# Rotary tables copied per block into DRAM, and a longer hold on addresses that stores read, in a decoder layer on eight cores

## The chip, the cores and the metric

The kernel runs on one Trainium2 chip, on 8 cores. Each core computes one sequence of the batch of eight; no core speaks to another. A core has five engines with a queue of instructions each: TensorE (PE, matrix products), VectorE (DVE), ScalarE (ACT), GpSimd (POOL) and SyncE (SP, which only issues transfers here), and 16 DMA engines that carry the transfers. Engines meet by semaphores. The metric is the device time in microseconds of the slowest core.

## The reference

One decoder layer for x of 4096 x 1024 per sequence, with a condition c that gives shifts, scales and gates (adaLN). A combined input projection feeds latent attention (8 heads, 96 = 64 plain + 32 rotary dimensions) and retention (4 heads), an output projection follows, then a SwiGLU feed-forward of width 2816.

```python
mod = (jax.nn.silu(c) @ w_ada[l] + b_ada[l])[:, None, :]
sh1, sc1, g1, sh2, sc2, g2 = jnp.split(mod, 6, axis=-1)
h = rmsnorm(x, pre_norm_mix[l]) * (1.0 + sc1) + sh1
z = h @ w_in[l]
cq, ckv, kpe, rq, rk, rv, rg = jnp.split(z, offsets, axis=-1)
y_mla = rmsnorm(mla_group(cq, ckv, kpe, positions, ...), mla_out_norm[l])
y_ret = retention_group(rq, rk, rv, rg, positions, ret_gn_gain[l])
mix = jnp.concatenate([y_mla, y_ret], axis=-1) @ w_out[l]
x = x + g1 * rmsnorm(mix, post_norm_mix[l])
h = rmsnorm(x, pre_norm_ffn[l]) * (1.0 + sc2) + sh2
f = (jax.nn.silu(h @ w_gate[l]) * (h @ w_up[l])) @ w_down[l]
x = x + g2 * rmsnorm(f, post_norm_ffn[l])
```

The part that the change touches is the rotary embedding of the queries. With cos and sin of position times frequency it is

```python
x1, x2 = jnp.split(x, 2, axis=-1)
jnp.concatenate([x1 * cos - x2 * sin, x1 * sin + x2 * cos], axis=-1)
```

## The kernel before

The sequence is cut into 8 blocks of 512 rows, and a block into 4 tiles of 128 rows. The program has three stages.

Projections: for `sb` from 0 to 7, `prep` loads and normalises four tiles of x (`xt`, `xn`) and turns them (`hT`), `z_part` multiplies them by the input weights `W1` (in the trace W and w) and forms per tile `cqn`, `ckn`, `kpn`, the rotated retention inputs (`r1`, `r2` in VectorE, both `r` in the trace, summed to `rqk`), `rv` and the gate (`th`, then `sg`). `latents` turns them and stores `cqT`, `ckT` and `kpT` to scratch in DRAM. `retention` of the block before runs between the tiles and stores `yn` to `yg_scr`, 128x512 f32, 256 KB a tile. `ada_chunk` computes one piece of the adaLN vectors per block from a 1 MB load `wadab`.

Attention: blocks in the order 6, 7, 5, 4, 3, 2, 1, 0. Keys are made from `ckTb` (loaded from `ck_scr`, a ring of 3) by `kgen`; queries of the next block by `qgen`, one of the fill steps between the score products. ScalarE takes the exponentials `PT`. Output projections of the block before fill the rest.

Feed-forward: blocks in the same order, products of `h2T` with `Wg`, `Wu`, and of `h1T` with `Wd`.

The rotary table of the queries: `angles` makes for all 4096 positions three tiles of 128x512 f32 (256 KB each), `fC` (cosine), `fS` (sine), `fN` (minus sine). Partition 16b + i holds frequency i for the 512 positions of block b. Each is stored whole to `tab_scr`. For a block, `load` in `qgen` fills `Cq` and `Sq`, 128x512 each: partition 32h + 16k + i is head h of four, half k, frequency i. For `Cq` both halves are the cosine, for `Sq` minus sine and sine. The table in DRAM has the 16 rows of a block once, so each of the two tiles is filled by 8 transfers of 16x512 (32 KB). `pe_part` multiplies two products by the two tables (`qt`, on VectorE), adds them (`qp`, on GpSimd), and four transfers carry the heads into `Q`.

Order and addresses: `record` writes the program down as a list of operations with the tiles that each reads and writes. From a first recording each tile has a life, from the first to the last operation that names it (`_touch`), and `_place` gives it an address in 212,800 bytes per partition: pinned and fixed tiles first, then by class (`cls`) and size. Small short-lived tiles are put where the addresses have been free for `GAPCAP` = 40 operations, if there is such a place. It tries seeds with random jitter until ten plans fit; each is recorded and ordered once, and the plan whose ordering the scheduler's cost table makes shortest is taken. `_list_schedule` orders each engine's queue with the same cost table: of the operations that are ready, the one recorded first. When a tile begins its life, its first writer waits for every operation that read or wrote a tile which had the same address (`b.alias`); for a tile that a transfer stores to DRAM that is the landing of the store. SyncE has 32 semaphores; its transfer number n (from 0) uses semaphore `ds_sp` n mod 32.

Of the kernel before, what the change touches and what calls it, by code (L numbers as in the profile page):

```python
# [9 lines left out]
F32 = mybir.dt.float32  # L10
# [10 lines left out]
NSB = 8  # L21
# [127 lines left out]
class Buf:  # L149
    def __init__(self, name, size, kind):  # L150
        self.name = name
        self.size = size
        self.kind = kind
        self.addr = 0
        self.first = None
        self.last = None
        self.whole = [None, []]
        self.subs = {}
        self.seen = False
        self.pin = False  # L160
        self.alias = None


class Sched:
# [61 lines left out]
    def op(self, eng, emit, r=(), w=(), dma=False):  # L226
        op = Op()
        op.eng = eng
        op.emit = _freeze(emit)
        op.is_dma = dma  # L230
        op.marked = False
        op.count = 0
        op.seq = len(self.order)
        d = set()
        rl = [k if isinstance(k, tuple) else (k, None) for k in r]
        wl = [k if isinstance(k, tuple) else (k, None) for k in w]
        for b, _ in rl + wl:
            self._touch(b, op.seq)

        def need(st, write, psum):  # L240
            if st[0] is not None:
                d.add(st[0])
            if write:
                d.update(st[1])
            elif psum:
                d.update(x for x in st[1] if x.eng != eng)

        for lst, write in ((rl, False), (wl, True)):
            for b, s in lst:
                ps = b.kind == "psum"  # L250
                need(b.whole, write, ps)
                if b.alias and b.whole[0] is None and (s is None or s not in b.subs or b.subs[s][0] is None):
                    d.update(b.alias)
                if s is None:
                    for st in b.subs.values():
                        need(st, write, ps)
                elif s in b.subs:
                    need(b.subs[s], write, ps)
        for b, s in rl:
            if s is None:  # L260
                b.whole[1].append(op)
            else:
                b.subs.setdefault(s, [None, []])[1].append(op)
        for b, s in wl:
            if s is None:
                b.whole = [op, []]
                b.subs = {}
            else:
                b.subs[s] = [op, []]
        d.discard(op)  # L270
        op.deps = d
        self.order.append(op)
        return op
# [8 lines left out]
    def _place(self, seed):  # L282
        rng = np.random.default_rng(seed)
        n = len(self.order)
        for b in self.bufs:
            if b.first is None:
                b.first = b.last = 0
            if b.pin:
                b.first, b.last = 0, n

        def cls(b):
            if b.pin or b.fix is not None:
                return -1 if b.fix is not None else 0
            if seed % 8 > 3 and b.last - b.first > 2000:
                return 0
            return 1 if b.last - b.first > (1000, 500, 1500, 250)[seed % 4] else 2

        jit = 1.0 + (0.5 * rng.random(len(self.bufs)) if seed else np.zeros(len(self.bufs)))
        order = sorted(self.bufs, key=lambda b: (cls(b), -b.size * (jit[b.no] if cls(b) == 1 else 1.0), b.first, b.no))
        m = len(order)  # L300
        A0, A1, L0, L1 = (np.zeros(m, np.int64) for _ in range(4))
        for i, b in enumerate(order):
            a0, a1, l0, l1 = A0[:i], A1[:i], L0[:i], L1[:i]
            live = (l0 <= b.last) & (l1 >= b.first)
            if b.fix is not None:
                b.addr = b.fix
                if (live & (a0 < b.addr + b.size) & (b.addr < a1)).any():
                    return f"{b.name} [{b.first},{b.last}] is not free at {b.addr}"
                A0[i], A1[i], L0[i], L1[i] = b.addr, b.addr + b.size, b.first, b.last
                continue  # L310
            cur, holes = 0, []
            for lo, hi in sorted(zip(a0[live].tolist(), a1[live].tolist())):
                if lo - cur >= b.size:
                    holes.append((cur, lo))
                cur = max(cur, hi)
            if ARENA - cur >= b.size:
                holes.append((cur, ARENA))
            if not holes:
                return f"no room for {b.name} {b.size} [{b.first},{b.last}]"
            near = (~live) & (l1 > b.first - GAPCAP) & (l0 < b.last + GAPCAP)  # L320
            na0, na1 = a0[near], a1[near]
            ngap = np.where(l1[near] < b.first, b.first - l1[near], l0[near] - b.last)
            edges = np.unique(np.concatenate([na1, na0 - b.size, a0[~live], a1[~live] - b.size]))
            best = None
            for lo, hi in holes:
                pts = np.unique(np.concatenate([[lo, hi - b.size], edges[(edges >= lo) & (edges <= hi - b.size)]]))
                if cls(b) == 2 and len(na0):
                    hit = (na0[None, :] < pts[:, None] + b.size) & (pts[:, None] < na1[None, :])
                    gap = np.minimum(np.where(hit, ngap[None, :], GAPCAP).min(axis=1), GAPCAP)
                else:  # L330
                    gap = np.full(len(pts), GAPCAP)
                edge = np.minimum(pts - lo, hi - b.size - pts)
                k = np.lexsort((pts, edge, -gap))[0]
                sc = (-int(gap[k]), int(edge[k]), int(pts[k]))
                if best is None or sc < best:
                    best = sc
            b.addr = best[2]
            A0[i], A1[i], L0[i], L1[i] = b.addr, b.addr + b.size, b.first, b.last
        plan = []
        for b in self.bufs:  # L340
            hit = (L1 < b.first) & (A0 < b.addr + b.size) & (b.addr < A1)
            over = sorted(order[k].no for k in np.nonzero(hit)[0])
            plan.append((b.addr, over))
        return plan
# [147 lines left out]


GAPCAP = 40


def bcast(v, dims):
# [6 lines left out]
def record(nc, S, dr, arena, psum):  # L504
# [249 lines left out]
    act(fS.v, fs_.v, AF.Sin, [fs_], [fS])  # L754
    act(fN.v, fs_.v, AF.Sin, [fs_], [fN], scale=-1.0)
    tabD = S.key("tabD")
    for i, t_ in enumerate((fC, fN, fS)):
        dma("sp", dr["tab"][i], t_.v, r=[t_], w=[(tabD, i)])

    Wvf = S.buf("Wvf", 2 * 512)  # L760
    dma("sp", Wvf.v.rearrange("p (c n) -> p c n", c=2), dr["wkv"][:, 512:1024].rearrange("(c p) n -> p c n", p=128), w=[Wvf])
# [263 lines left out]
    def qgen(s, engs=("dve", "dve")):  # L1025
# [11 lines left out]
        def load():  # L1037
            box["C"] = rg["Cq"]()
            box["S"] = rg["Sq"]()
            for k, o in (("C", [0, 0]), ("S", [1, 2])):  # L1040
                for hf in range(2):
                    for hd in range(4):
                        p0 = hd * 32 + hf * 16
                        dma("sp", box[k].v[p0:p0 + 16, :], dr["tab"][o[hf]][s * 16:(s + 1) * 16, :], r=[(tabD, o[hf])], w=[(box[k], p0)])

        def pe_part(q4):
            def a():
# [49 lines left out]
    for sb in range(NSB):  # L1097
        R = {}
        if sb > 0:
            ada_load(ada_list[sb])  # L1100
        if sb + 1 < NSB:
            hT2, xst, trs = prep(sb + 1, load_x(sb + 1))
        zset[0] = (2, 3, 4, 5, 6, 7) if sb == 0 else (2, 3, 4, 5, 6)
        zg = [z_part(sb, hT, R, j) for j in range(4)]
        for j in range(4):
            if j == 3 and sb + 1 < NSB:
                trs()
            for _ in range(4):
                for g_ in (zg if sb == 0 else zg[j:j + 1]):
                    next(g_, None)  # L1110
                if sb == 0:
                    break
            if prev:
                retention(*prev, j)
            if sb == NSB - 1:
                early_keys(j)
            if sb == 0 and j == 1:
                ada_load(ada_list[0])
            if j < 2 and sb + 1 < NSB:
                xst(2 * j)  # L1120
                xst(2 * j + 1)
        if sb == NSB - 2:
            first.extend(qgen(order[0], AD))
            first[1][0]()
        ada_chunk(ada_list[sb])
        if sb == 5:
            b_weights()
        res = []
        lat = latents(sb, R, res)
        if sb + 1 < NSB:  # L1130
            for _ in lat:
                pass
            prev = (sb, R) + tuple(res)
        hT = hT2
# [314 lines left out]
def build_nc():  # L1449
# [30 lines left out]
    dr["cqT"] = nc.dram_tensor("cq_scr", [NSB, 128, 3 * 512], BF16).ap()  # L1480
    dr["ckT"] = nc.dram_tensor("ck_scr", [NSB, 128, 2 * 512], BF16).ap()
    dr["kpT"] = nc.dram_tensor("kp_scr", [32, T], BF16).ap()
    dr["tab"] = nc.dram_tensor("tab_scr", [3, 128, 512], F32).ap()

    with contextlib.ExitStack() as ctx:
        arena = ctx.enter_context(nc.sbuf_tensor("arena", [128, ARENA // 4], F32))
# [113 lines left out]
```

How the kernel before makes its waits and increments, by code:

```python
    def then_inc(self, *a, **kw):  # L145
        return self
# [324 lines left out]
        def run(e, engobj):  # L471
            for op in self.ops[e]:
                for d in op.waits:
                    if d.is_dma:
                        n = NSEM[d.eng]
                        engobj.wait_ge(dsem[d.eng][d.dma_i % n], 16 * (d.dma_i // n + 1))
                    else:
                        engobj.wait_ge(esem[d.eng], d.count)
                ins = op.emit(engobj)
                if op.is_dma:
                    ins.then_inc(dsem[e][op.dma_i % NSEM[e]], 16)
                elif op.marked:
                    if ins is None:
                        ins = engobj.nop()
                    ins.then_inc(esem[e], 1)
```

## Time and profile before

| | us |
|---|---|
| median of 3 runs | 2051.67 |
| lowest, highest | 2024.93, 2135.98 |
| profiled execution | 2027.99 |
| its span (slowest core, core 2) | 2026.4 |
| spans of the eight cores | 2005.9 to 2026.4 |
| TensorE busy | 1854.3 (92%) |
| ScalarE busy | 965.1 (48%) |
| VectorE busy | 808.4 (40%) |
| GpSimd busy | 627.1 (31%) |
| moved by DMA | 189.71 MB, mean 94 GB/s |

The page divides the span into engine times, a chain of work that ended last, and groups of instructions. The chain lies 71% on TensorE, 9% on DMA, 8% on ScalarE and 3% on SyncE's queue; the store of `yn` to `yg_scr` alone has 3% of it. The mean granted clock of TensorE is 0.984 on the slowest core and 0.984 to 0.989 over the eight. Idle time is read as "idle before an instruction, and who released it"; a wait for several semaphores is put down to the one that came last.

### The profile page before, as it was taken

What the parts mean: (1) busy time and instruction counts of PE and PEld (TensorE: products, weight loads), DVE (VectorE), ACT (ScalarE), POOL (GpSimd) and SP (SyncE); (2) the same over time, 40 slices, a digit from 0 to 9 for tenths busy, and PEclk for the clock granted to TensorE, in tenths of its full rate; (3) what the DMA queues carried; (4) which work ended last, traced back from release to release, by engine and by line L of the source; (5) the groups of instructions that cost most, each with busy time, mean ns of one, the idle gap of its engine ahead of it and who ended that gap; (6) DMA issues with size and microseconds to landing.
All of it is one profiled execution on the core that took longest, in us unless ns stands there. A gap on an engine that the chain in (4) does not pass through costs nothing.

```text
span 2026.4 us, 38698 instructions; the slowest of 8 cores (2005.9 to 2026.4 us)
## 1 busy us (share of the span) xinstructions
PE 1854.3 (92%) x13325; PEld 973.1 (48%) x13536; DVE 808.4 (40%) x1733; ACT 965.1 (48%) x1449; POOL 627.1 (31%) x939
## 2 busy tenths in 40 slices
PE   1799988979989899999989999999999999999998
PEld 1355545535555555565544444444444444444443
DVE  4455655555444143545785423131221313122111
ACT  3566666539989999998741122121211212121111
POOL 3345546531523133435673330120302021020202
PEclk9999999989999999999989999999999999999999
DMA  9945445453323233254488621120202011120101
GB/s 251 170 97 127 124 119 139 85 117 90 94 79 105 40 100 88 82 121 129 121 196 180 161 97 44 52 73 22 104 11 83 32 57 68 42 84 22 53 22 63
DMA packets 91495, 189.71 MB, mean 94 GB/s; under 512 B 9640, under 2 KB 39976, under 8 KB 91304
## 3 DMA queue, kind: packets, MB, share of 16 engines
q1 hardware_dynamic: 62392, 157.02, 24.5%
q0 software_dynamic: 28912, 30.21, 9.9%
q8 instruction: 112, 1.84, 0.4%
q14 instruction: 79, 0.65, 0.1%
HBM read 167.34 MB, written 47.97 MB: 106 GB/s over the span
## 4 chain that ended last, share of the span: by engine, by line
PE 71%; DMA 9%; ACT 8%; issue 5%; SPq 3%; DVE 2%; POOL 1%; DVEq 0%; POOLq 0%; ACTq 0%
PE bank L541 69%; ACT PT L517 7%; DMA yg_scr<-yn 3%; SPq L514 3%; PE bank L548 2%; DMA W<-w 2%; DMA waf<-w_ada 1%; DMA yg<-yg_scr 1%; DMA xa<-x_scr 0%; ACT yn L517 0%; DMA ckTb<-ck_scr 0%; DMA cq_scr<-cqT 0%; POOL yn L520 0%; DVE mo L533 0%; DVE Q L533 0%
## 5 line engine op out<-in xcount | busy, mean ns | idle before, releaser
L517 ACT ACTIVATE PT<-bank 128x1024 bf16<-128x1024 f32 (+1 forms) x538 | 516.8, 1012 | 62.5 <-PE bank L541 51.1
L541 PE MATMUL bank<-Q,KT 96*128 96x512 bf16 (+3 forms) x1152 | 319.1, 364 | 27.0 <-ACT PT L517 13.2
L517 ACT ACTIVATE sgt<-bank 128x512 bf16<-128x512 f32 x176 | 104.8, 597 | 491.9 <-PE bank L541 445.7
L541 PE MATMUL bank<-h2T,Wg 128*128 128x512 bf16 x1396 | 332.7, 380 | 3.6 <-ACT sgt L517 2.5
L541 PE MATMUL bank<-h2T,Wu 128*128 128x512 bf16 x1357 | 326.8, 379 | 2.6
L541 PEld LDWEIGHTS bank<-V,PT 128*128 128x128 bf16 x4224 | 235.4, 97 | 173.5 <-issue 13.0
L541 PE MATMUL bank<-Wd,h1T 128*128 128x512 bf16 x1382 | 306.3, 379 | 1.7 <-DVE mo L533 0.4
L520 DVE TENSOR_TENSOR h1T<-bank,sgt 128x512 bf16<-128x512 f32 x176 | 121.3, 690 | 427.7 <-PE bank L541 396.4
L541 PE MATMUL bank<-W,hT 128*128 128x512 bf16 (+2 forms) x1252 | 257.5, 358 | 25.7 <-DVE r L520 8.8
L541 PE MATMUL bank<-V,PT 128*128 128x65 bf16 x4224 | 268.6, 193 | 6.3 <-POOL PT L520 2.9
L541 PEld LDWEIGHTS bank<-h2T,Wg 128*128 128x128 bf16 x1408 | 137.4, 98 | 168.6 <-issue 5.9
L541 PEld LDWEIGHTS bank<-Wd,h1T 128*128 128x128 bf16 x1408 | 137.6, 98 | 166.3 <-issue 0.9
L541 PEld LDWEIGHTS bank<-h2T,Wu 128*128 128x128 bf16 x1408 | 137.4, 98 | 164.2
L520 POOL TENSOR_TENSOR st<-st 128x1 f32<-128x1 f32 x32 | 6.2, 195 | 605.3 <-ACT t L517 605.3
L541 PEld LDWEIGHTS bank<-W,hT 128*128 128x128 bf16 x1280 | 123.5, 100 | 139.2 <-issue 40.1
L517 ACT ACTIVATE t<-bank 128x512 f32<-128x512 f32 x64 | 38.2, 597 | 276.7 <-PE bank L541 236.9
L520 POOL TENSOR_TENSOR PT<-PT,trib 128x256 bf16<-128x256 bf16 (+1 forms) x160 | 94.6, 595 | 236.1 <-ACT PT L517 232.0
L541 PE MATMUL bank<-Wo,yT 128*128 128x512 bf16 x461 | 141.2, 381 | 4.5 <-ACT PT L517 1.4
L528 DVE SCALAR_TENSOR_TENSOR t<-bank,st,G2b 128x512 f32<-128x512 f32 x64 | 45.1, 746 | 235.8 <-POOL st L520 235.8
L541 PEld LDWEIGHTS bank<-Q,KT 96*128 96x128 bf16 x1152 | 80.9, 97 | 62.1 <-issue 45.9
L520 POOL TENSOR_TENSOR xt<-xt,mo 128x512 f32<-128x512 f32 x64 | 88.2, 1394 | 25.1 <-DVE mo L528 24.3
L520 POOL TENSOR_TENSOR xb<-xb,t 128x512 f32<-128x512 f32 x64 | 80.6, 1281 | 28.2 <-DVE t L528 27.6
(160 smaller groups left out, 1847.0 us busy)
## 6 DMA issues: line engine op xcount, KB each, us to landing
xt<-x SPq DMA_DIRECT2D x64, 512.0 KB, 5.4
x_scr<-xt SPq DMA_DIRECT2D x32, 512.0 KB, 2.7
xa<-x_scr SPq DMA_DIRECT2D x32, 512.0 KB, 4.5
xb<-x_scr SPq DMA_DIRECT2D x32, 512.0 KB, 3.5
out<-xb SPq DMA_DIRECT2D x32, 512.0 KB, 2.6
waf<-w_ada SPq DMA_DIRECT2D x4, 2048.0 KB, 21.1
wadab<-w_ada POOLq DMA_DIRECT2D x8, 1024.0 KB, 14.2
yg_scr<-yn SPq DMA_DIRECT2D x32, 256.0 KB, 3.1
```

The source lines that it names most:

```text
L514: return OP(q, lambda g: g.dma_start(out=out, in_=in_), r, w, dma=True)
L517: return OP("act", lambda g: g.activation(out=out, in_=in_, func=func, **kw), r, w)
L520: return OP(eng, lambda g: g.tensor_tensor(out=out, in0=a, in1=b, op=op), r, w)
L528: return OP("dve", lambda g: g.scalar_tensor_tensor(out=out, in0=a, scalar=sc, in1=b, op0=op0, op1=op1), r, w)
L541: x = g.matmul(out, lhsT=l, rhs=rh, start=st, stop=sp, **kw)
L548: x = g.transpose(out=out, in_=i, identity=identb.v)
```

## The change

Three things change. The table in DRAM becomes two tables of 8 blocks x 128 rows x 512, in the layout of `Cq` and `Sq`; `store_tables` fills them by 16 stores of 8 x 16 x 512 (256 KB each), from the same three tiles, which are kept until then. It is recorded in block 2 and names a part of `V1` as read, so it can't run before that part of block 1 is written. `load` takes each table of a block with one transfer of 128x512. And a tile whose last use is a transfer that reads it keeps its address for `STORE` = 60 more operations of the list. The class by which large long-lived tiles are placed is also split in two by size for some seeds.

```diff
+        if dma:
+            for b, _ in rl:
+                b.stored = op.seq
...
             if b.pin:
                 b.first, b.last = 0, n
+            elif b.stored == b.last:
+                b.last = min(n, b.last + STORE)
+                b.stored = -1
...
             if seed % 8 > 3 and b.last - b.first > 2000:
-                return 0
+                return 0.25 if b.size >= 8192 else 0.5
...
+STORE = 60
...
-    for i, t_ in enumerate((fC, fN, fS)):
-        dma("sp", dr["tab"][i], t_.v, r=[t_], w=[(tabD, i)])
+    def store_tables():
+        for k, hf, t_ in ((0, 0, fC), (0, 1, fC), (1, 0, fN), (1, 1, fS)):
+            for hd in range(4):
+                dma("sp", bass.AP(dr["tab"].tensor, (k * NSB * 128 + hd * 32 + hf * 16) * 512, [[128 * 512, NSB], [512, 16], [1, 512]]), t_.v,
+                    r=[t_, (Vt[1], 3)], w=[(tabD, (k, hf, hd))])
...
-            for k, o in (("C", [0, 0]), ("S", [1, 2])):
-                for hf in range(2):
-                    for hd in range(4):
-                        p0 = hd * 32 + hf * 16
-                        dma("sp", box[k].v[p0:p0 + 16, :], dr["tab"][o[hf]][s * 16:(s + 1) * 16, :], r=[(tabD, o[hf])], w=[(box[k], p0)])
+            for i, k in enumerate("CS"):
+                dma("sp", box[k].v, dr["tab"][i, s], r=[tabD], w=[box[k]])
...
+        if sb == 2:
+            store_tables()
...
-    dr["tab"] = nc.dram_tensor("tab_scr", [3, 128, 512], F32).ap()
+    dr["tab"] = nc.dram_tensor("tab_scr", [2, NSB, 128, 512], F32).ap()
```

SyncE's queue at the end of block 1, before. The names are the stores of `latents` and `retention` and the loads of x:

```order
L514 DMA yg_scr<-yn 128x512
L514 DMA ck_scr<-ckT 128x1024
L514 DMA cq_scr<-cqT 128x1536
L514 DMA xt<-x 128x1024
L514 DMA kp_scr<-kpT 32x512
L514 DMA yg_scr<-yn 128x512 x3
```

and of the changed kernel at the same place:

```order
L522 DMA yg_scr<-yn 128x512
L522 DMA ck_scr<-ckT 128x1024
L522 DMA tab_scr<-fC 8x16x512
L522 DMA cq_scr<-cqT 128x1536
L522 DMA tab_scr<-fC 8x16x512
L522 DMA kp_scr<-kpT 32x512
L522 DMA tab_scr<-fC 8x16x512 x6
L522 DMA tab_scr<-fN 8x16x512
L522 DMA yg_scr<-yn 128x512
L522 DMA tab_scr<-fN 8x16x512 x3
L522 DMA tab_scr<-fS 8x16x512 x4
L522 DMA yg_scr<-yn 128x512 x2
```

The sixteen table stores stand in between, nine of them ahead of the first `yn` store of the next tiles. The three stores of before stood ahead of the x loads of block 1.

VectorE's queue in the first tile of block 2, before. `r1_291` and `r2_292` are the two rotary products; semaphore 9 of SyncE is there that of transfer 41, the store of `yn_270`:

```order
L520 TENSOR_TENSOR r1_291<-bank1,Ct_95 128x512 [waits es_pe]
L520 TENSOR_TENSOR rv_286<-bank1,wk_81 128x512 [waits es_pe,ds_sp18]
L524 TENSOR_SCALAR ckn_283<-bank3,lst_281 128x256 [waits es_pool]
L520 TENSOR_TENSOR scm_294<-bank2,Dm_80 128x512 [waits es_pe]
L528 SCALAR_TENSOR_TENSOR sg_287<-th_293,bank2 128x512 [waits es_act,ds_sp23]
L520 TENSOR_TENSOR r2_292<-bank1,St_96 128x512 [waits ds_sp9]
```

and of the changed kernel:

```order
L528 TENSOR_TENSOR r2_292<-bank1,St_96 128x512 [waits es_pe]
L528 TENSOR_TENSOR kp1_289<-bank3,Ct_95 128x32 [waits es_act]
L528 TENSOR_TENSOR kp2_290<-bank3,St_96 128x32
L528 TENSOR_TENSOR rv_286<-bank1,wk_81 128x512 [waits es_pe]
L532 TENSOR_SCALAR ckn_283<-bank3,lst_281 128x256 [waits es_pool]
L528 TENSOR_TENSOR r1_291<-bank1,Ct_95 128x512 [waits ds_sp2]
```

`r2_292` no longer waits for a transfer; `r1_291` now waits for one, number 34, the store of `yn_252`, one tile older. On ScalarE the next tile's `th_313` waited for TensorE alone and now also for transfer 47 (semaphore 15), the store of `yn_270`:

```order
L525 ACTIVATE xn_279,xst_320<-xt_278 128x1024 [waits ds_sp31]
L525 ACTIVATE yn_298<-bank3,gs_297 128x128 [waits es_dve]
L525 ACTIVATE yn_298<-bank3,gs_297 128x128 x3
L525 ACTIVATE th_313<-bank3 128x512 [waits es_pe,ds_sp15]
L525 ACTIVATE xn_279<-xt_277,xst_319 128x1024 [waits es_act,es_pool]
```

## Rows read from the trace of the kernel before

**Rows 1.** Part 1 of the page: busy us, share of the span, instructions, by engine.

```profile
PE 1854.3 (92%) x13325; PEld 973.1 (48%) x13536; DVE 808.4 (40%) x1733; ACT 965.1 (48%) x1449; POOL 627.1 (31%) x939
```

**Rows 2.** Core 2 by stage: length; PE, PEld, DVE, ACT, POOL busy; clock; DMA share; GB/s.

```profile
0.00:90.00 90.00, 32.30 (x286) 19.82 (x288) 42.63 (x72) 40.49 (x65) 32.87 (x50) 0.99 1.01 230
...
145.00:370.00 225.00, 201.71 (x1453) 115.51 (x1474) 129.04 (x402) 141.14 (x298) 124.57 (x208) 0.97 0.48 124
...
370.00:470.00 100.00, 78.94 (x513) 40.33 (x520) 57.50 (x151) 49.65 (x100) 38.92 (x55) 0.91 0.50 109
...
470.00:1060.00 590.00, 542.59 (x6144) 328.77 (x6223) 295.11 (x617) 519.28 (x560) 237.17 (x330) 0.98 0.39 104
...
1165.00:1990.00 825.00, 820.89 (x3912) 380.90 (x3989) 192.66 (x294) 159.24 (x322) 120.06 (x192) 1.00 0.16 54
```

**Rows 3.** Waits, 90 to 450 us: total us, times, longest.

```profile
DVE r L520 <- DMA yg_scr<-yn: 13.4, 4, 4.2
...
PE bank L541 <- DVE r L520: 8.8, 6, 2.6
...
ACT xn L517 <- DMA kp_scr<-kpT: 8.8, 2, 5.2
...
ACT xn L517 <- DMA cq_scr<-cqT: 7.2, 3, 3.1
...
ACT yn L517 <- DMA yg_scr<-yn: 6.5, 3, 4.8
...
POOL Wq L525 <- DMA yg_scr<-yn: 5.1, 1, 5.1
```

**Rows 4.** Timeline, VectorE and TensorE: start, us, instruction, [idle before <- releaser].

```profile
162.96 0.69 DVE L520 TENSOR_TENSOR r<-bank,St 128x512 f32<-128x512 f32 x1 [3.07 <-DMA yg_scr<-yn]
...
163.79 5.89 PE L541 MATMUL bank<-W,hT 128*128 128x384 bf16 x32 [1.81 <-DVE r L520]
```

**Rows 5.** The chain of work that ended last, 150 to 170 us: start, us, what.

```profile
156.68 6.18 DMA yg_scr<-yn
```

**Rows 6.** Timeline of SyncE's queue, 405 to 442 us.

```profile
420.16 5.26 SPq L514 DMA_DIRECT2D Cq<-tab_scr  x8
...
425.56 0.31 SPq L514 DMA_DIRECT2D Sq<-tab_scr  x1
...
428.53 2.85 SPq L514 DMA_DIRECT2D Sq<-tab_scr  x6
...
431.88 0.43 SPq L514 DMA_DIRECT2D Sq<-tab_scr  x1
...
441.65 0.35 SPq L514 DMA_DIRECT2D ckTb<-ck_scr  x1
```

**Rows 7.** Timeline of TensorE, 395 to 470 us.

```profile
441.65 1.87 PE L541 MATMUL bank<-ckTb,Wk 128*128 128x512 bf16 x4 [3.33 <-DMA ckTb<-ck_scr]
...
445.92 1.01 PE L541 MATMUL bank<-ckTb,Wk 128*128 128x512 bf16 x2 [2.41 <-DVE KT L533]
...
449.84 4.03 PE L541 MATMUL bank<-ckTb,Wk 128*128 128x512 bf16 x10 [2.91 <-DMA ckTb<-ck_scr]
```

**Rows 8.** Timeline of the head: SyncE's first table store, TensorE's last wait.

```profile
63.76 0.33 SPq L514 DMA_DIRECT2D tab_scr<-fS  x1
...
90.14 7.70 PE L541 MATMUL bank<-W,hT 128*128 128x512 bf16 x24 [6.03 <-DMA W<-w]
```

**Rows 9.** Busy time of the stage from 80 to 90 us, columns as in rows 2.

```profile
80.00:90.00 10.00, 4.06 (x19) 1.67 (x17) 2.07 (x3) 6.58 (x10) 4.32 (x10) 0.91 1.05 254
```

**Rows 10.** DMA issues, 90 to 450 us: count, KB each, median us to landing.

```profile
yg_scr<-yn SPq DMA_DIRECT2D x27, 256.0 KB, 4.4
```

**Rows 11.** The tile Sq: who waited for it (us, times).

```profile
  DVE qt L520: 5.8, 1
```

**Rows 12.** Timeline of SyncE's queue and ScalarE in the second block.

```profile
149.50 0.33 SPq L514 DMA_DIRECT2D ck_scr<-ckT  x1
...
171.98 0.61 ACT L517 ACTIVATE th<-bank 128x512 f32<-128x512 f32 x1
...
188.69 0.82 SPq L514 DMA_DIRECT2D xt<-x  x2
```

More of the change, by code:

```diff
@@ L161, in __init__ @@
         self.alias = None
+        self.stored = -1
 class Sched:
```

## The prediction

> **What bounds the kernel now.** I read the busy shares first, then the busy time by stage, then the waits and the timeline of the stages in which TensorE stands idle. TensorE is busy in 92% of the span [rows 1]. By stage [rows 2], it is busy 820.89 of the last 825 us, so nothing can pay there; before that its idle time is 57.7 us in the first 90 us (loads of weights), 225 - 201.71 = 23.3 us from 145 to 370 (the projections and the retention), 100 - 78.94 = 21.1 us from 370 to 470 (the last projection block and the start of attention), and 47.4 us in the 590 us of attention that follow, where ScalarE is itself busy 519.28 us of 590, so that a table load moved there can give little. The granted clock is 0.97 and 0.91 in the two stages that the change touches most.
>
> In the projection stage other engines wait for stores to land [rows 3]: VectorE's rotary products 13.4 us in four waits, ScalarE 8.8, 7.2 and 6.5 us, GpSimd 5.1 us, 41 us in all. They aren't data waits: the waiting instruction writes an address which a store still reads. TensorE in turn waits for VectorE's `r` 8.8 us in six waits. One of them in full [rows 4, 5]: the store of `yn` is issued at 156.68 and takes 6.18 us; the `r` product starts at 162.96 after 3.07 us of idleness, and TensorE at 163.79 after 1.81 us. So a 3 us wait on VectorE cost TensorE about 1.8.
>
> At the start of attention SyncE's queue is a chain of issues [rows 6]: from 420.16 on eight pieces of Cq (5.26 us), one of Sq (0.31), six more (2.85) and so on, with other issues between, until the key latent load goes out at 441.65. TensorE waits 3.33, 2.41 and 2.91 us there [rows 7], two of the three directly for such loads.
>
> **The change, part by part.** The sum is made against the profiled execution, 2028.0 us (span 2026.4), which lies 24 us under the median of the three runs (2051.67) and 3 us above the fastest (2024.93).
>
> *Three table stores leave the head.* They were 0.79 MB, issued from 63.76 on, in a stage in which the DMA engines are busy without a break until the last projection weight lands at 90.14 [rows 8]. At the 254 GB/s of the last ten microseconds [rows 9], 0.79 MB is 3.1 us. Against it, the x loads of the next blocks no longer stand behind ScalarE's sines and can start sooner; two more of them (1.0 MB) ahead of the weights would cost 4.1 us. Gain 2; bounds 3.1 gained and 1.0 lost.
>
> *Addresses are held for sixty more instructions.* The reuse that followed a store by some forty recorded instructions now follows it by at least a hundred, in a stage that records about sixty instructions per 128 rows and spends 225 us on some twenty such tiles, about 11 us each. A store lands in 4.4 us in the median there [rows 10], so the shortest reuses go from under to over its landing. Of the 41 us, nearly all should go; TensorE can regain what it waits for `r`, 8.8 us at most directly, and not all its 23.3 us of idleness, of which the rest ends on products, transposes and norms. By the ratio of [rows 4] I take 6 us. The clock at 0.97 over 225 us means some 13 us at the lower level (1.2 of 2.4 GHz), which cost half of that; fewer gaps may give back 2. Gain 8; bounds 0 and 23.3 + 6.7 = 30.
>
> *Two table loads instead of sixteen per block.* Bytes stay (2 x 256 KB). SyncE saves 14 issues a block. In the stage of [rows 6] sixteen pieces take 5.26 + 0.31 + 2.85 + 0.43 (the last piece) = 8.85 us of the queue, two whole loads 0.7, so what stands behind them can go 8 us sooner, and the stores of `yn` that SyncE and ScalarE wait for there fall out too. TensorE's three waits sum to 8.65 us; with part of it tied to the copies between, I take 5, and 2 for the clock (0.91 over 100 us is 18 us at the lower level, which cost 9). Gain 7; bounds 0 and 21.1 + 9 = 30. Later in attention the only wait for a table is VectorE's 5.8 us, once [rows 11], with none on TensorE behind it: gain 1, bounds 0 and 5.8. Where a whole load replaces the piece that an early product needed, nothing is lost, since the product reads all 128 partitions anyway.
>
> *Sixteen stores of 256 KB in the second block.* They write 4.19 MB in place of 0.79. In the new order the first ones stand right behind the ck store, which was issued at 149.50 [rows 12], the bulk behind the kp store, and nine of them ahead of the store of `yn_270`, whose address ScalarE's `th_313` now reuses. At 254 GB/s one takes 1.03 us. The seven behind the kp store, queued from about 153.3 on, end at 160.5, and with 4.4 us for its own way the `yn` store is down at 164.9. `th` of that tile ran at 171.98 [rows 12]. So it is covered by 7 us, and all sixteen are through by about 171, before the next x loads (188.69). SyncE's extra sixteen issues (5 us at 0.33 each) lie in a stretch where it waits for `yn`. I take a cost of 1; bounds 0 and, if every one took the 4.4 us of [rows 10] in turn, ten (with the `yn` store itself) x 4.4 = 44 us, landing at 193.5 and 22 late.
>
> *The address plan* is drawn anew and moves the order of single instructions on all engines. I see no row that prices this; it is worth nothing either way in the sum, and in the range up to the 9 us that all waits for `r` make.
>
> Sum: -2 - 8 - 7 - 1 + 1 = -17 us, 2028 - 17 = **2011 us**.
>
> **The rivals.**
>
> *A: the new stores run on half of the DMA engines* (0.17). Each goes out as 8 blocks x 16 rows on the DRAM side, where all the old ones had 128 rows outermost. At half rate one takes 2.06 us, seven end at 153.3 + 14.4 = 167.7, the `yn` store lands at 172.1, level with `th`'s old time and up to 8 us behind it where the tiles ahead have moved up. ScalarE's queue, with the norms and casts behind it, would stand for 0 to 8 us, and the `w_ada` load meanwhile shares the loaded engines. Cost 4 more: 2015 us. No row here shows a transfer of this shape with its landing. The Trainium skill, "DMA: Bandwidth & Descriptors", section on why a DMA increments its semaphore by 16, states that the slowest dimension of both sides sets how many engines take part, which here would be 8. By that rule the sum would be 2015, by the rate of the rows 2011; no run here has shown it yet.
>
> *B: the waits only change their name* (0.22). For it speaks that in 145 to 370 only 8.8 of 23.3 idle us are behind `r`, and that several store waits lie on ScalarE beside other waits. A freed engine then stops at the next product, and the key loads at the start of attention wait for their rings instead. Gain 2 of the head at most, 2026 us.
>
> *C: the gaps go as a whole* (0.15). The chain of waits passes through stores again and again in the first stages; if two thirds of 23.3 + 21.1 us vanish (-30) and half of the clock's 16 us comes back (-8), it is 1990 us.
>
> *D: slower* (0.08). The mechanism is the queue of sixteen stores alone: in turn at 4.4 us each, `th_313` stands 22 us, and x loads issued behind them come late into the same gap. 2011 - 1 + 22 = 2032, with a gain of only half elsewhere 2040. It decides from 18 us of lateness on, which is (171.98 + 18 - 149.5) / 10 = 4.0 us a store.
>
> **How the numbers follow.** Forecast 0.38, A 0.17, B 0.22, C 0.15, D 0.08. The likeliest is 2011, its own range 1998 to 2024. The range from 1988 to 2042 takes in A and B, most of C, and D up to near its upper end; it also holds executions a little above the profiled one, as one of the three runs was. Two per cent is about what a measurement of this kernel can tell from no change. Against the profiled time the line is 1987, below which only part of C lies; against the median it is 2011, and which of these the comparison comes near depends on its runs. I give 0.17 for faster, 0.04 for slower (D with a mean start), 0.79 between.
>
> **What would show it.** In the profile after: VectorE's and ScalarE's waits for yg, cq and kp stores between 90 and 450 us under 12 us in all (they were 41); TensorE's idleness from 145 to 370 about 16 us and the clock at 0.98 or more; W's last wait ended near 88 us; the key latent loads at the start of attention issued 6 to 8 us sooner by the same mark and TensorE's idleness in those 100 us near 15; a wait of ScalarE's `th` for the yn store near 165 us absent (present means A or D, and the landing of the table stores tells which). The forecast is wrong if idleness in these stages stays within 5 us of what it was, or if it falls but attention, with the redrawn plan, takes it back.

## The result, and the profile after

The changed kernel takes 2012.13 us in the median, against 2027.94 for the kernel before, measured beside it. The ratio is 0.9936, 95% interval 0.9918 to 0.9955: faster, by less than 2%. The forecast was 2011 us. The number was right, in part by luck: several of its terms were not, and another address plan of the same kernel comes out near 1995 us, as shown below.

| | before | after |
|---|---|---|
| median, us | 2027.94 | 2012.13 |
| profiled execution | 2027.99 | 2021.09 |
| spans of cores 0 to 3 | 2007.7 to 2026.4 | 1987.7 to 2003.0 |
| moved by DMA, MB | 189.71 | 193.10 |

In 8 of the 18 executions of after that the ratio counts, the profiled one among them (there on cores 4 to 7), some cores ran at a granted clock of 0.968 to 0.976 and took longer, so all rows of after are from cores 0 to 3, and the other ten executions have a median of 2006.6 us. The view by core has the span and clock:

```profile
core 2: 1988.1 us, clock 0.988
...
core 7: 2017.6 us, clock 0.973
```

Core 2 by stage, the same view as in [rows 2]. The columns are length; PE, PEld, DVE, ACT and POOL busy with instruction counts; clock; DMA share; GB/s:

```profile
0.00:90.00 90.00, 37.43 (x300) 21.56 (x301) 42.28 (x73) 41.83 (x67) 28.28 (x52) 0.97 1.01 233
145.00:370.00 225.00, 209.36 (x1553) 120.01 (x1551) 135.35 (x426) 148.00 (x314) 130.87 (x215) 0.98 0.51 142
370.00:470.00 100.00, 85.15 (x642) 44.09 (x641) 62.74 (x137) 60.63 (x101) 31.05 (x46) 0.93 0.45 113
470.00:1060.00 590.00, 556.62 (x6167) 331.61 (x6165) 302.74 (x637) 503.06 (x545) 248.07 (x344) 0.99 0.43 112
1135.00:1960.00 825.00, 825.00 (x3991) 380.81 (x3989) 192.48 (x294) 159.35 (x324) 118.42 (x197) 1.00 0.16 54
```

TensorE's idleness on this core went from 23.3 to 225 - 209.36 = 15.6 us in the projections, from 21.1 to 14.9 at the start of attention, and from 47.4 to 33.4 in attention. The last is the largest fall, in the stage to which the prediction gave 1 us.

The waits for stores from 90 to 450 us on core 2, the same view as in [rows 3] (total us, times, longest), are these two:

```profile
ACT xn L525 <- DMA ck_scr<-ckT: 4.5, 3, 2.1
...
ACT th L525 <- DMA yg_scr<-yn: 3.6, 1, 3.6
```

and one of VectorE's `r` of 0.8 us: 8.9 us, where there were 41. TensorE's 8.8 us of waits for `r` are gone.

**A ledger that doesn't depend on the clock time.** Fixed windows cut the two programs at different work. So I also read at what time TensorE starts its weight load number n. There are 13,536 of them on each core and in every kernel here. Number 500 lies in the second block, 3000 in the first attention block, 9000 near the end of attention; the end is the last weight load. Medians, us from one mark to the next, over the eight cores before and over cores 0 to 3 after:

| | 0 to 500 | 500 to 3000 | 3000 to 9000 | 9000 to end |
|---|---|---|---|---|
| before | 116.8 | 369.3 | 572.7 | 944.2 |
| after | 115.3 | 365.5 | 561.0 | 942.4 |
| difference | -1.5 | -3.8 | -11.7 | -1.8 |
| predicted | -2 | -14 | -1 | 0 |

Over cores 0 to 3 on both sides the differences are -1.6, -5.1, -12.6 and -2.0.

Cores of one execution do the same work, yet from 500 to 3000 they differ by 8 us before (368.2 to 376.0) and by 10 after (360.2 to 370.4). Core 2 went from 376.0 to 360.2, so it alone would suggest a gain of 16 us where the medians give 4.

### The profile page after: what moved, and what is told of

Same layout as the page of the kernel before. It is cut to its first block, busy times and chain, and to the rows that moved or that the text cites. A ratio compares the mean times of both kernels' runs of the same rounds, so it can differ in the third digit from the quotient of the medians.

```text
span 2019.5 us, 38646 instructions; the slowest of 8 cores (1987.7 to 2019.5 us)
## 1 busy us (share of the span) xinstructions
PE 1883.3 (93%) x13536; PEld 979.8 (49%) x13536; DVE 809.6 (40%) x1733; ACT 966.3 (48%) x1449; POOL 615.9 (30%) x939
## 2 busy tenths in 40 slices
DMA packets 91445, 193.10 MB, mean 96 GB/s; under 512 B 7928, under 2 KB 38264, under 8 KB 91256
## 4 chain that ended last, share of the span: by engine, by line
PE 77%; ACT 8%; DMA 7%; issue 3%; SPq 2%; DVE 1%; POOL 1%; POOLq 0%; ACTq 0%; DVEq 0%
PE bank L549 75%; ACT PT L525 7%; PE bank L556 2%; DMA W<-w 2%; SPq L522 2%; DMA yg_scr<-yn 1%; DMA waf<-w_ada 1%; DMA ckTb<-ck_scr 1%; DMA xt<-x 0%; DMA xa<-x_scr 0%; DMA ck_scr<-ckT 0%; DMA bb<-b_ada 0%; DMA wstage<-wq 0%; DVE Q L541 0%; DVE mo L541 0%
## 5 line engine op out<-in xcount | busy, mean ns | idle before, releaser
L549 PE MATMUL bank<-h2T,Wu 128*128 128x512 bf16 x1408 | 332.6, 379 | 0.0
L549 PE MATMUL bank<-W,hT 128*128 128x512 bf16 (+2 forms) x1280 | 277.6, 376 | 20.3 <-DMA W<-w 7.4
L549 PEld LDWEIGHTS bank<-W,hT 128*128 128x128 bf16 x1280 | 128.5, 103 | 144.3 <-issue 69.5
L549 PE MATMUL bank<-Wo,yT 128*128 128x512 bf16 x512 | 159.0, 385 | 2.4 <-DVE mo L541 1.2
L533 POOL TENSOR_SCALAR xst<-xst 128x1 f32<-128x1 f32 x64 | 12.5, 195 | 256.9 <-ACT xn L525 255.3
```

The lines of the kernel that those rows point to most:

```text
L533: return OP(eng, lambda g: g.tensor_scalar(out=out, in0=a, scalar1=s1, scalar2=s2, op0=op0, op1=op1), r, w)
L549: x = g.matmul(out, lhsT=l, rhs=rh, start=st, stop=sp, **kw)
```

## The experiments

Twelve kernels ran, each against the kernel before on the same chip. The marks are medians over eight cores, for the change and for "both" over cores 0 to 3. "Store waits" are the waits of all engines for the stores of `yn`, `cqT`, `ckT` and `kpT` from 90 to 450 us, lowest and highest of cores 0 to 3.

| kernel | ratio, interval | 500 to 3000 | 3000 to 9000 | store waits |
|---|---|---|---|---|
| before | 1 | 369.3 | 572.7 | 35 to 44 |
| before, other plan | 0.996 (0.9945, 0.9975) | 368.0 | 572.5 | 25 to 41 |
| hold alone | 0.9953 (0.9935, 0.9972) | 364.6 | 570.0 | 6 to 21 |
| hold alone, other plan | 1.0033 (1.0007, 1.006) | 373.3 | 573.8 | 3 to 17 |
| tables alone | 0.9928 (0.9904, 0.9953) | 368.8 | 559.9 | 32 to 44 |
| tables alone, other plan | 0.9997 (0.9975, 1.0019) | 388.7 | 561.8 | 26 to 28 |
| the change | 0.9936 (0.9918, 0.9955) | 365.5 | 561.0 | 6 to 12 |
| the change, second plan | 0.9836 (0.9803, 0.9869) | 359.1 | 561.3 | 7 to 15 |
| the change, third plan | 0.987 (0.9844, 0.9896) | 359.0 | 561.0 | 4 to 11 |
| change, stores led by 16 | 0.9907 (0.9882, 0.9931) | 364.7 | 560.6 | 5 to 15 |
| "both": second plan, led by 16 | 0.9853 (0.9835, 0.9872) | 360.4 | 562.6 | 9 to 27 |
| led by 16, over two blocks | 0.9841 (0.982, 0.9863) | 358.9 | 559.7 | 4 to 14 |
| change, two pieces a table | 0.9927 (0.99, 0.9954) | 365.1 | 560.7 | 12 to 17 |
| change, eight pieces a table | 0.9942 (0.992, 0.9965) | 360.2 | 574.6 | 9 to 15 |

**The hold alone, the tables alone, and the plan.** The theory (H): the hold takes the store waits away and the tables do the rest. The rival (L): what moves the time is the address plan drawn anew.

```diff
 # hold alone: before.py with these lines of the change, and those that set b.stored
+                b.last = min(n, b.last + STORE)
+STORE = 60
 # tables alone: the changed kernel
-STORE = 60
+STORE = 0
 # another plan
-        for plan in itertools.islice(S0.place(), 10):
+        for plan in itertools.islice(S0.place(), 10, 20):
```

> The kernel before with the hold of sixty operations alone; table stores and loads as before. Theory H (the hold removes the waits for stores in the projections, the tables do the rest): VectorE's, ScalarE's and GpSimd's waits for yg, cq and kp stores fall from 41 us under 12, the projections end 8 to 10 us sooner, the start of attention keeps its sixteen pieces and gains nothing; about 0.9955 of the time before. Theory L (what the change gives is the address plan drawn anew, not the hold): the waits may fall, but the time is as likely over as under that of before, between 0.996 and 1.004.

> The changed kernel with the hold set to 0 operations: stored tables, sixteen stores in block 2 and two loads a block. Theory H: the waits for stores between 90 and 450 us stand at some 35 to 41 us again, the head keeps its 4 us, the stretch around the sixteen stores loses 7, and attention gains some 10 to 13 (no wait for Sq, shorter SyncE queue): about 0.995 to 0.998. If the gain of attention belongs to the hold and not to the tables, attention takes as long as before and the time is 1.000 to 1.003.

> The kernel before, whose address plan is chosen from the second ten plans that fit in place of the first ten; nothing else changes. Theory H: no gain, 0.999 to 1.003, and the waits for stores stay near 41 us. Theory L: it moves by as much as the change did, up to 6 us per thousand either way, and single waits such as the 5.8 us for Sq in attention come or go with the plan.

Of the kernel before only eleven plans fit at all, so the redraw took the eleventh (the kernel itself has the fifth). The hold does to the waits what it should: 6 to 21 us in place of 35 to 44. But the plan alone, with the waits in place, gains as much time (0.996 against 0.9953). The tables alone, with all store waits in place, gain as much as the whole change. So neither theory is enough, and each part needed a second plan:

```diff
 # hold alone, other plan: the seventh of nine, not the eighth
-        for plan in itertools.islice(S0.place(), 10):
+        for plan in itertools.islice(S0.place(), 7):
 # the change (second plan): the eleventh of eleven, not the eighth; tables alone: the twelfth of twelve
+        for plan in itertools.islice(S0.place(), 10, 20):
 # the change (third plan): the fourth of eleven
+        for plan in itertools.islice(S0.place(), 7):
```

> The kernel before with the hold of sixty operations, as in the first run of this study, but with another of the nine address plans that fit. If the hold pays by the waits that it takes away: 0.995 again, within 0.001 or 0.002 of the first, and waits for stores under 20 us. If the address plan decides: it lands between 0.993 and 1.000, away from 0.9953, with the waits for stores as low.

> The changed kernel with another of its eleven address plans, nothing else changed. Attention from weight load 3000 to 9000 stays at 561 us, since the two loads set it. The two waits of xn for x of 11 us together near 200 us, for tiles whose address a store of yn still reads, belong to the plan and can be gone: then 1100 to 1300 takes 30 to 34 us and not 36 to 38, and the time is 0.990 to 0.993. If they are not the plan's, the time stays at 0.9936.

> The changed kernel without the hold, as in the second run of this study, with another address plan. If two loads instead of sixteen pay about 10 us whatever the plan: attention at 560 to 562 us from weight load 3000 to 9000, waits for stores 30 to 45 us, and a time of 0.991 to 0.997. If the 0.9928 of the second run was a lucky plan as a whole, attention too goes back to 570 and the time to 0.998 or more.

> The changed kernel with a third of its eleven address plans. Attention stays at 559 to 563 us from weight load 3000 to 9000; the waits for stores stay under 20 us; the time is between 0.983 and 0.997, by what single waits the plan makes before 300 us. A time outside of that would say that a plan moves more than the 10 us per thousand seen so far.

The plans of one kernel differ by 0.4 to 1.0% of the time, 8 to 20 us; the change itself moved 13. Even so, each of the three plans of the change (0.9836 to 0.9936) came out faster than both plans of the kernel before (0.996 and 1; the nearest two have intervals that just overlap), while the hold alone and the tables alone, over their two plans, lie at 0.9993 and 0.9963 in the mean. That speaks for a gain that comes only with both. The largest single waits can be named, though not all of the time is in them. The hold with its other plan is 373.3 - 364.6 = 9 us slower from 500 to 3000, and from 2300 to 3000 alone 17 (124.6 against 108.0). Core 2 of it, timeline of SyncE, VectorE and TensorE:

```profile
357.73 3.56 SPq L522 DMA_DIRECT2D Sq<-tab_scr  x8
361.45 0.35 SPq L522 DMA_DIRECT2D gp<-gpost  x1
362.00 0.35 SPq L522 DMA_DIRECT2D bb<-b_ada  x1
...
370.60 0.69 DVE L528 TENSOR_TENSOR bb<-bank,bb 128x512 f32<-128x512 f32 x1 [8.33 <-DMA bb<-b_ada]
...
372.16 1.44 PE L556 MATMUL bank<-identb,cqn 128*128 128x128 bf16 x12 [7.19 <-DVE rqBD L541]
```

A small load stands behind the sixteen table pieces (the eight for `Cq` go out just ahead, from 353.90), VectorE waits 8.33 us for it, and TensorE 7.19 us for what stands behind that on VectorE. That the pieces are the cause isn't shown. The load goes out at 362.00, no later than in other kernels (363.12 in the change, 371.36 on core 2 before, where nothing waits for it); but it takes 8.5 us to land, and in this plan its reader stands in VectorE's queue at 362.3. The wait is also less than half of the 17 us; the granted clock from 360 to 380 us was 0.83.

Tables without the hold lose most in 500 to 3000 in the other plan (388.7 against 368.8, and 0.9997 in all where at most 0.997 was expected). With the sixteen stores in block 2, the `yn` stores that the waits are for take longer to land. Core 0 of it, timeline:

```profile
166.26 1.06 ACT L525 ACTIVATE xn<-xt 128x1024 bf16<-128x1024 f32 x1 [5.26 <-DMA yg_scr<-yn]
...
177.13 0.69 DVE L528 TENSOR_TENSOR r<-bank,Ct 128x512 f32<-128x512 f32 x1 [4.22 <-DMA yg_scr<-yn]
...
178.56 5.49 PE L549 MATMUL bank<-W,hT 128*128 128x384 bf16 x16 [4.25 <-DVE r L528]
```

and the landing of its three `yn` stores of that stretch, shortest, median, longest:

```profile
DMA to landing us min/median/max: 2.0/9.9/10.0
```

against a median of 4.1 to 5.2 in the same stretch on cores 0 to 3 before. From mark 500 to 1300, where these waits lie, tables alone take 118.0 and 122.1 us in the two plans, and the kernel before 107.5 and 115.6. So these waits are at most 4 of the 20 us between the two plans of tables alone; 12.5 lie from 1300 to 2300 and 3 from 2300 to 3000, and their cause stays open. The hold may be worth more where the stores are. The table goes with that, and does not prove it: hold and stores together take 358.9 to 365.5 us from 500 to 3000 in all eight kernels that have both, and the six that lack one or both take 364.6 to 388.7, five of them 368 or more. How much of this is the pairing and how much the plans, two plans each can't say.

In the change as it was made, the same kind of single wait costs time as well. Core 2 of after:

```profile
186.17 0.33 SPq L522 DMA_DIRECT2D yg_scr<-yn  x1
...
194.21 0.33 SPq L522 DMA_DIRECT2D xt<-x  x1
...
195.33 0.33 SPq L522 DMA_DIRECT2D xt<-x  x1
...
199.68 1.06 ACT L525 ACTIVATE xn<-xt 128x1024 bf16<-128x1024 f32 x1 [6.21 <-DMA xt<-x]
...
201.44 0.59 PE L549 MATMUL bank<-rqBD,rkT 128*128 128x256 bf16 x2 [4.24 <-ACT cqn L525]
205.91 1.06 ACT L525 ACTIVATE xn<-xt 128x1024 bf16<-128x1024 f32 x1 [4.62 <-DMA xt<-x]
```

The third x load goes out 8 us after the issue of a `yn` store. It waits for that store's semaphore, as the rows of SyncE's queue in the program show, since its tile has the address of `yn_338`:

```
L522 DMA yg_scr<-yn_338 128x512 [waits es_pool,ds_sp27]
L522 DMA ck_scr<-ckT_358 128x1024 [waits es_act,ds_sp28]
L522 DMA xt_362<-x 128x1024 [waits ds_sp27,ds_sp1]
```

The hold of sixty recorded operations did not prevent this: what is sixty operations later in the list can stand two places later in SyncE's queue. TensorE takes 36.2 us from mark 1100 to 1300 in the change, 29.7 before, and 28.1 and 28.0 in the second and third plan, which have no wait for x at that place: all four x loads of the block stand ahead of that store. That was expected of the second plan; that it gains 20 us and not 1 to 7 was not. Against the 2006.6 us above it would be some 12, and the ledger has 8, of which 6 lie from 500 to 3000.

The split of the class of large tiles did nothing: with and without it the changed kernel is the same program, addresses included.

**Pieces against whole loads.** The attention term is the one that no plan touches: 559.7 to 562.6 us in every kernel with whole tables, 570.0 to 573.8 in the four with sixteen pieces from the old table. Is it the loads, or the new layout in DRAM, which came with them?

```diff
-                dma("sp", box[k].v, dr["tab"][i, s], r=[tabD], w=[box[k]])
+                for p0 in range(0, 128, 16):
+                    dma("sp", box[k].v[p0:p0 + 16, :], dr["tab"][i, s, p0:p0 + 16, :], r=[tabD], w=[(box[k], p0)])
 # two pieces a table: 64 in place of 16
```

> The changed kernel with each table of a block loaded by eight transfers of 16x512 instead of one of 128x512; the table in DRAM, the sixteen stores and the hold stay. Theory P (the gain of 10 to 12 us in attention comes from the fewer issues in SyncE's queue): attention, from weight load 3000 to 9000 of TensorE, takes 570 us again instead of 561, the 4 to 6 us wait of qt for Sq is back, and the time rises by 8 to 12 us to that of 0.998. Rival: the gain came from the layout or from the plan; then attention stays at 561 and the time at 0.9936.

> The changed kernel with each table of a block loaded in two transfers of 64x512: four issues per block instead of two or sixteen. If the cost of the pieces is the time of their issues in SyncE's queue (0.32 us each), attention from weight load 3000 to 9000 takes 562 to 563 us, an eighth of the 12 us on top of 561. If splitting a table at all costs (a second piece queued behind other stores), it takes 565 to 572 us.

Eight pieces a table take attention back to 574.6, two leave it at 560.7. So the gain is the loads', not the layout's; a second piece costs nothing (560.7, where 562 to 563 was expected of the issues alone), and sixteen a block cost 13.6 us. The kernel with eight pieces lost less in all than expected (0.9942), since its plan is 5 us quicker from 500 to 3000 than that of the change. That the wait for `Sq` would return was wrong: in this plan the late one behind the pieces is another. Core 1 of the kernel with eight pieces, timeline:

```profile
535.79 0.84 SPq L522 DMA_DIRECT2D Sq<-tab_scr  x2
536.68 0.88 SPq L522 DMA_DIRECT2D yg<-yg_scr  x2
539.06 0.32 SPq L522 DMA_DIRECT2D cqTb<-cq_scr  x1
...
542.61 0.59 PE L549 MATMUL bank<-cqTb,Wq 128*128 128x512 bf16 x2 [2.18 <-DMA cqTb<-cq_scr]
543.85 4.21 ACT L525 ACTIVATE PT<-bank 128x1024 bf16<-128x1024 f32 x4 [2.43 <-PE bank L549]
```

And the same place in the kernel before, core 2, which the prediction had read in part only:

```profile
555.96 3.77 SPq L514 DMA_DIRECT2D Sq<-tab_scr  x6
...
559.82 2.42 SPq L514 DMA_DIRECT2D Q<-qp  x4
562.40 0.48 SPq L514 DMA_DIRECT2D wstage<-wout  x1
562.93 0.88 SPq L514 DMA_DIRECT2D Sq<-tab_scr  x2
...
566.68 0.69 DVE L520 TENSOR_TENSOR qt<-bank,Sq 128x512 f32<-128x512 f32 x1 [5.76 <-DMA Sq<-tab_scr]
567.29 0.17 DVE L1367 RECIPROCAL rd<-bank 128x4 f32<-128x4 f32 x1
567.52 0.59 PE L541 MATMUL bank<-cqTb,Wq 128*128 128x512 bf16 x1 [3.83 <-DVE rd L1367]
...
569.27 1.02 ACT L517 ACTIVATE PT<-bank 128x1024 bf16<-128x1024 f32 x1 [4.80 <-PE bank L541]
```

The last two pieces of `Sq` go out behind the four transfers of the heads into `Q` and a weight load. VectorE waits 5.76 us, then does `qt` and `rd`; TensorE waits 3.83 us for `rd`, and ScalarE, the busiest engine after TensorE here, stands 4.80 us. The 100 weight loads around it (3700 to 3800) took 14.8 us and take 8.4 in after. From 3500 to 4000 the five kernels with sixteen pieces take 49.1 to 50.6 us and the nine others 43.4 to 44.8: 7 of the 12 us lie there. The rest is at few places too, 1.2 us at 5900 and 1.9 to 3.6 us at 8000 (cores 1 and 2); most blocks gain nothing.

**Half of the DMA engines.** Rival A said that stores whose DRAM side is led by 8 blocks run at half rate. The same stores, led by 16 rows:

```diff
-  [[128 * 512, NSB], [512, 16], [1, 512]]), t_.v,
+  [[512, 16], [128 * 512, NSB], [1, 512]]), t_.v,
```

with the positions and frequencies of the tables laid out to match (partition 8i + b in place of 16b + i).

> The changed kernel with the DRAM side of the sixteen stores led by 16 rows and not by 8 blocks (the table's rows in SBUF are arranged to fit); bytes, number and place of the stores are the same. Rival A of the prediction (the stores ran on half of the DMA engines): their stretch from 147 to 168 us shortens by some 6 to 8 us, ScalarE's 3.6 us wait of th and the waits for x at 200 us shrink, the time falls by 3 to 7 us against the changed kernel (about 0.991). If the bytes alone count: the stretch stays 20 us long and the time is that of the changed kernel (0.9936).

Same plan, same bytes. Core 2 in two stretches of 5 us, in the changed kernel:

```profile
155.00:160.00 5.00, 5.00 (x31) 2.58 (x30) 3.51 (x14) 4.61 (x11) 3.42 (x9) 1.00 0.69 230
160.00:165.00 5.00, 5.00 (x34) 2.81 (x33) 2.47 (x5) 2.77 (x7) 3.89 (x6) 1.00 0.54 200
```

and with the stores led by 16:

```profile
155.00:160.00 5.00, 4.95 (x29) 2.42 (x28) 3.83 (x15) 4.85 (x12) 3.75 (x9) 1.00 1.08 275
160.00:165.00 5.00, 4.95 (x32) 2.80 (x32) 2.83 (x5) 3.84 (x8) 3.58 (x6) 1.00 1.04 381
```

The DMA share is 0.54 with the queue full, and 1.04 when the shape is turned (0.52 to 0.61 and 1.04 to 1.08 on cores 0 to 3, from 160 to 165 us; the view can come out a little over 1 when all are busy): half of the engines stood idle. SyncE's issues show it as well, each held back by the full queue (times of one in ns, lowest, median, highest; the changed kernel first):

```profile
L522 SPq DMA_DIRECT2D tab_scr<-fS x4: 1071/1434/1704, 161.8 to 166.3; - x4
```

```profile
L522 SPq DMA_DIRECT2D tab_scr<-fS x4: 600/708/1490, 159.0 to 162.0; - x4
```

The Trainium skill, "DMA: Bandwidth & Descriptors", section on why a DMA increments its semaphore by 16, has this rule (the slowest dimension of both sides sets the number of engines), and this case's trace agrees: 0.54 against 1.04 of the engines. The wait that it caused is there too, on ScalarE in the changed kernel, where the prediction said that it would be under A:

```profile
166.41 0.60 ACT L525 ACTIVATE th<-bank 128x512 f32<-128x512 f32 x1 [3.64 <-DMA yg_scr<-yn]
```

It is 1.16 us with the stores led by 16. In time no gain is shown: 0.9907 against 0.9936, with intervals that overlap, and 364.7 against 365.5 us from 500 to 3000. The stretch of the stores shortened by 4.6 us (from 146.7 to 167.6 us, then from 146.3 to 162.6), where 6 to 8 were expected, and the waits for x at 200 us did not shrink as expected (8.1 to 11.1 us on cores 0 to 3 before the turn, 9.7 to 14.7 after); the second and third plan, which have none, show that they are the plan's. The last two kernels put the parts together:

> The changed kernel with the address plan of the seventh run and the sixteen stores led by 16 rows as in the fourth. The two gains lie in different places (the stores' stretch from 145 to 170 us; the waits for x near 200 us) and should add: 0.9836 less 0.002 to 0.003, so 0.981, with the landing of the yn store near 6 us instead of 8 in 145 to 190 us. If the layout's gain depended on the plan, it stays at 0.983 to 0.985.

> The changed kernel with stores led by 16 rows, eight of them recorded in block 2 and eight in block 3, and a plan of its own. If the sixteen stores in a row still cost in the form with 16 rows (they take the DMA engines from 145 to 165 us): yn stores land in 5 us or less in 145 to 190 us, and the time is 2 to 4 us under that of the fourth run of this study (0.9907), 0.989. If they no longer cost, only the plan speaks, 0.981 to 0.995.

On the second plan the turned stores gave nothing (0.9853, 0.9836 without), though the `yn` stores from 145 to 190 us landed in 2.3 to 6.2 us in place of 8.2 to 10.1 (medians of cores 0 to 3). Spread over blocks 2 and 3 they gave 0.9841, in a plan of their own; but the `yn` stores landed in 5.2 to 9.5 us there (medians of cores 0 to 3), where 5 or less was expected, so the time can't be put down to the spreading. The best time measured is 0.9836, with 0.9841 and 0.9853 too close to it to be told apart. Both halves of the expectation "the two gains should add" fell: one of them is too small to be seen behind the other.

## Why the prediction was right, and where it wasn't

**The sum was right because two errors cancel, and that is luck.** The medians of the ledger add up to -18.8, the timed median of the slowest cores fell by 13 (0.64% of 2028), and the forecast was -17. It gave 14 us to the stage from 500 to 3000, which brought 3.8 in this plan (10 in the other two), and 1 us to attention, which brought 11.7. The plan was luck as well: with the other two the same change comes to 0.987 and 0.9836 of the time before, some 2002 and 1995 us.

**Head, -2.** Measured -1.5. The last W wait ended at 85.32 on core 2, where [rows 8] has 90.14; 88 was forecast. The range over cores 0 to 3 is 85.3 to 90.5, and was 85.6 to 92.1. From 0 to 500 the four kernels with the table stores in the head take 115.5 to 123.1 us and the ten without 111.9 to 118.3, so the term is right in size and not much more can be said.

**The hold, -8.** The step "of the 41 us, nearly all should go" held in every kernel with the hold: 3 to 27 us are left. The step from there to TensorE's time did not. Alone, the hold came out at -9.5 us (0.9953) with one plan and +6.7 (1.0033) with another, both times with most of the waits gone and TensorE's wait for `r` at 0 on cores 0 to 3. In the second plan VectorE waits 8.33 us for a small load instead, which is rival B; why that load came late for its reader is not settled. The term can't be given a size of its own from these runs; together with the stores in block 2 the stage was shorter than before in each of the eight kernels.

**SyncE's issues at the start of attention, -7.** Here the place was wrong. The key loads do go out sooner: from 416.86 us on core 2, 4 us behind the end of the last projection product (412.7), where the load at 441.65 [rows 6] stood 9 behind it (433.0). That is 4.5 us sooner, and 6 to 8 were forecast. But TensorE's wait for them did not go away:

```profile
425.52 4.06 PE L549 MATMUL bank<-ckTb,Wk 128*128 128x512 bf16 x10 [7.47 <-DMA ckTb<-ck_scr]
```

It waits 9.9 us for `ckTb` in all, in [rows 7] 3.33 + 2.91 = 6.2. From mark 2300 to 3000 it took 109.7 us before, 106.1 before with the other plan, 107.3 after, and 107.4 in the kernel with the sixteen pieces put back. So of the 7 us about 2 came, and nothing shows that the fewer issues brought them. The forecasts for the fixed windows (idleness of 16 and 15 us, clock 0.98) were met with 15.6, 14.9 and 0.98, but on a core that had been the slowest of its execution there.

**Later table loads, -1.** The failed step is "the only wait for a table is VectorE's 5.8 us, once [rows 11], with none on TensorE behind it". The wait of TensorE behind it carries the name of `rd`, the next instruction in VectorE's queue, not of `qt`. That one place is 6 to 7 us, about the upper bound of the term. The others (5900, 8000) had no wait for a table to point at them. In all it is 12 us, by 572.7 against 561.0, and 13.6 by the comparison of 574.6 with 561.0. The bound "0 and 5.8" was drawn from the one wait with a table's name, so it left out everything that stood behind the pieces. This is the term with the largest miss, and the only one that was the same in every plan.

**Sixteen stores, +1.** The cover of 7 us that `th` had was not there: it waited 3.64 us, the sign of A. But the store landed at 166.4, between the forecast's 164.9 and A's 172.1; what took the cover away is `th`, which was ready at 162.8 and not at 171.98, since the work ahead of it had moved up by 9 us. The half rate was shown, its cost was not: 0 to 6 us. Rival D (22 us late) fell, as the `yn` store landed within 10.5 us.

**The plan, 0 in the sum and up to 9 in the range.** This was the mis-sized bound. Two plans of one kernel differed by 8 us (before), 16 (hold), 14 (tables) and 20 (the change, 0.9936 and 0.9836). The change as measured had the poorest of its three plans, in part through two waits for x (36.2 us against 28.1 and 28.0 from 1100 to 1300) which the prediction did not see, because it looked only for waits that go, and not for tiles that the new plan puts in the place of a stored one.

## What to carry to other kernels

Sixteen small pieces in place of two loads took 6 to 8 us more of the issuing queue at each block, and the price was paid only where something late stood behind them, at some three places of attention here: count the issues between a late load and the end of its predecessor, and follow the waiting engine's next instruction, since the wait downstream carries that one's name. Where an edit makes a planner draw its addresses anew, measure each variant with two or three plans before a gain of under 1% is credited to the edit. And a store that is written for its layout is better led by 16 rows than by 8 blocks, where both are possible; here it doubled the rate of the stores, though no time was gained that can be shown.

## What was not expected of the hardware

Cores of one chip that run the same program on data of the same size differ by 7 to 21 us in the same stage (351.5 to 366.8 us from mark 500 to 3000 in the kernel with spread stores, 348.3 to 367.5 in the third plan), while attention differs by 1 to 6. The stage with the many waits for transfers takes a different time on each core, and the slowest one makes the metric, so comparing one core with one core there is worth nothing under some 10 us.

A transfer led by 8 blocks took half of the DMA engines, and the other transfers were slower beside it too: the median landing of the `yn` stores from 145 to 190 us was 8.3 to 9.8 us on cores 0 to 3 with it, 5.9 to 7.3 with the shape turned, and 4.1 to 5.2 without the table stores.
